# Three adding transfers in place of two for the low parts of an up slab, in a two-layer hybrid decoder trunk

## The chip, the cores and the metric

The kernel runs on one core of a Trainium2 chip. The metric is the device time of one execution, in microseconds (us); lower is better. Before the change the median of three runs is 1875.01 us (1873.65 to 1876.04).

## The reference, cut to what matters

The model has two layers over 528 tokens (16 learned meta tokens and 512 input tokens) of width 1024. Each layer is a mixing half (a convolution branch beside differential attention, gated and projected) and an MLP. Only the MLP is touched by the change:

```python
u = rms_norm(h, norm_mlp[l])
h = h + jnp.square(jax.nn.relu(u @ w_up[l])) @ w_down[l]     # w_up 1024 x 4096, w_down 4096 x 1024
...
return h[:, N_META:N_META + S]
```

All weights are float32. The kernel gets that precision from a faster matmul type (fp32r): a weight w is held as a high part, w rounded to fp32r, and a low part, w minus its high part, and so are the activations. A product is then three matmuls: high x high, high x low, low x high.

## The kernel before, in words

**Slabs.** All weights come as slabs of 1 MB (128 partitions x 2048 float32), 144 over both layers, by one transfer each into one of two buffers of `w_raw` (L604). A slab's high parts go to `w_hi`, its low parts to `w_lo`. In the MLP of a layer four groups g = 0..3 follow each other, each with four up slabs (m = 0..3) and then four down slabs (d = 0..3). Slab m uses buffer m % 2 everywhere.

**Up slabs.** An up slab holds four blocks of weights of 256 KB (QUAD = 512 columns each). `up_products` (L846, matmuls on L883) multiplies them in Winograd's form of Strassen's scheme: seven products in place of eight, in the order p1, p5, p2, p6, p7, p4, p3. Each product is 12 matmuls (four chunks of the inner dimension, three matmuls each), so a slab is 84. p1 takes block 0 of `w_hi`/`w_lo`, p5 block 1, p2 block 2, p6 block 3. The other three products take `x_hi`/`x_lo`, which hold three further blocks: a plain one, then two sums. PE (TensorE) waits for the low parts, for the high parts (`w_form`) and for the sums of the slab before (`u2_done`) ahead of p1; for `p1_done` (ACT's copy of p1) ahead of p6; for `late_low` (the first of the two summed blocks in `x_lo`) ahead of p7; and for `w_ready` (all of `x_lo`) ahead of p3.

**Low parts of an up slab.** ACT (ScalarE) writes minus the weights into `w_lo` (`early_neg`, L1224 for three blocks, L1225 for the last, which is a sum `s2` made by DVE). Later ACT writes `w_hi` (`early_high`, L1230 and L1231). POOL (GpSimd) then issues, in `early_low` (L728), transfers that add the weights to `w_lo` in flight, with rounding to fp32r: w_lo = fp32r(-w) + w. Ahead of them it runs a tiny instruction `tick` (L734) and waits for it. The other low parts, `x_lo`, are subtractions on POOL itself: `late_parts` (L738, L747), four instructions of 128 columns for the plain block and eight for the two sums. POOL's order in a group g > 0 is written out (L750 to L770): early_low(1), plain(1), early_low(2), sums(1), plain(2), early_low(3), sums(2), plain(3) and sums(3), then the four down slabs' low parts (L634, 16 subtractions each), then early_low and late_parts of slab 0 of the next group.

**What waits for the low parts.** Both transfers of a slab signal the semaphore `low_landed[b]`, 16 each. PE waits for both ahead of p1 (L852). SP (SyncE) waits for both at L597, and for `w_form`, `late_low` and `sum_late`, before it loads slab m + 2 into the same buffer of `w_raw`. DVE (VectorE) makes the sums `s2` (L1960, L1961) once a slab has landed, and the sums `s34` for `x_lo` (L1972, L1973) once POOL has read the ones before. ACT's work around a slab of the up stage is, in order: first_product (L1252), hidden_high of the slab before (L1258, L1259), late_plain (L1238), early_high, early_neg of the slab after the next, late_sums (L1244), hidden_high. `down_high` (L1325) follows for the down slabs.

Of the kernel before, what the change touches and what calls it, by code (L numbers as in the profile page):

```python
# [26 lines left out]
ALU = mybir.AluOpType  # L27
# [27 lines left out]
SLAB = NT * 2 * P  # L55
# [14 lines left out]
QUAD = SLAB // 4  # L70
# [209 lines left out]
def build(nc, x_t, w_slabs, pvecs, rows_in, ident_in, mask_in, identb_in, out, h_spill, r_rows):  # L280
    ctx = ExitStack()
    with ctx:
        sem = lambda name: ctx.enter_context(nc.semaphore(name))
# [71 lines left out]
        s2 = at("s2", [P, 2, QUAD], F32, c); c += 2 * QUAD * 4  # L355
# [9 lines left out]
        w_raw = at("w_raw", [P, 2, SLAB], F32, r_w)  # L365
# [78 lines left out]
        u_raw, t_raw, f_hi, f_ready = sem("u_raw"), sem("t_raw"), sem("f_hi"), sem("f_ready")  # L444
        sum_early, sum_late, sums_read = sem("sum_early"), sem("sum_late"), sem("sums_read")
        w_neg, w_form, w_late = sem("w_neg"), sem("w_form"), sem("w_late")
        low_landed, late_low = [sem("low_landed0"), sem("low_landed1")], sem("late_low")
        q_full, p1_done, u2_done, c22_done, tile_sum, relu_done = (sem(x) for x in ("q_full", "p1_done", "u2_done", "c22_done", "tile_sum", "relu_done"))
        v_chain, a_chain, p_chain = sem("v_chain"), sem("a_chain"), sem("p_chain")

# [119 lines left out]
        @block.sync  # L570
        def _(sp):
            slabs = w_slabs.rearrange("(i b) p c -> b i p c", b=2)
            for k, landed in enumerate(h_landed):
                if k in (1, 2):
                    half = slice((k - 1) * SLAB // 2, k * SLAB // 2)
                    sp.dma_start(w_raw[:, 0, half], slabs[0, 0, :, half]).then_inc(w_landed[0] if k == 2 else half_landed, 16)
                sp.dma_start(h[:, 2 * k:2 * k + 2, :], x_t[:, 2 * k:2 * k + 2, :]).then_inc(landed, 16)
            for dst, src in ((ident, ident_in), (maskb, mask_in), (identb, identb_in)):
                sp.dma_start(dst[:], src).then_inc(in_landed, 16)
            sp.dma_start(w_raw[:, 1, :], slabs[1, 0]).then_inc(w_landed[1], 16)  # L580

            def load_slabs(first, last):

                with sp.Fori(first // 2, last // 2) as i:
                    for b in range(2):
                        sp.wait_ge(w_ready, 2 * i + (b - 1))
                        sp.dma_start(w_raw[:, b, :], slabs[b, ds(i, 1)].rearrange("o p c -> p (o c)")).then_inc(w_landed[b], 16)

            start = 2
            for layer in range(LAYERS):  # L590
                load_slabs(start, up_slab(layer, 0, 2))
                for g in range(4):
                    for m in range(8):
                        s = up_slab(layer, g, m + 2)
                        if m < 4:
                            n = up_nth(layer, g, m)
                            sp.wait_ge(low_landed[n % 2], 32 * (n // 2 + 1))  # L597
                            sp.wait_ge(w_form, n + 1)
                            sp.wait_ge(late_low, 2 * n + 1)
                            sp.wait_ge(sum_late, n + 1)  # L600
                        else:
                            sp.wait_ge(w_ready, s - 1)
                        if s < LAYERS * SLABS:
                            sp.dma_start(w_raw[:, s % 2, :], slabs[s % 2, s // 2]).then_inc(w_landed[s % 2], 16)  # L604
                start = (layer + 1) * SLABS + 2
            for i in range(NT):

                sp.wait_ge(h_new, (LAYERS - 1) * NT + i + 1)
                sp.dma_start(out[:, i, :], h[:, i, META:T]).then_inc(stored, 16)
            sp.wait_ge(stored, 16 * NT)  # L610
# [3 lines left out]
        def _(pool):  # L614
# [73 lines left out]
            for layer in range(LAYERS):  # L688
                s0 = layer * SLABS + S_QKV
                splits(done, s0 // 2)  # L690
                split(0, s0 // 2)
                split(1, s0 // 2)
                taps = head_taps(layer)
                for s in range(s0 + 2, s0 + N_QKV + 2):
                    pair, x = (s - 2 - s0) // 3, (s - 2 - s0) % 3 - 1

                    if x == 0:
                        if pair:

                            pool.wait_ge(p_ready, layer * HEADS + 2 * pair - 1)  # L700
                        turn(layer, pair, 0)
                    elif x == 1:

                        pool.wait_ge(scaled, layer * 4 + pair + 1)
                        turn(layer, pair, 1)

                        if pair in (1, 2):
                            pool.wait_ge(roped, (layer * 4 + pair) * 2 + 2)
                    elif pair in range(1, 4):

                        pool.wait_ge(max_ready, (layer * HEADS + 2 * pair - 2) * 3 + 1)
                    split_low(s % 2, s // 2, layer * N_HIGH + s - 1 - s0)
                    if x < 0:
                        for _ in range(4):
                            next(taps, None)
                for _ in taps:
                    pass
                splits((s0 + N_QKV + 2) // 2, (layer * SLABS + S_PW) // 2)
                for m in range(N_PW + N_O):
                    s = layer * SLABS + S_PW + m  # L720
                    split_low(s % 2, s // 2, layer * N_HIGH + N_QKV + m + 1)

                def down_low(g, d):

                    s = down_slab(layer, g, d)
                    split_low(s % 2, s // 2, layer * N_HIGH + N_QKV + N_PW + N_O + 4 * g + d + 1)

                def early_low(g, m):  # L728

                    b, n = m % 2, up_nth(layer, g, m)  # L730
                    pool.wait_ge(w_neg, n + 1)
                    if n > 1:
                        pool.wait_ge(low_landed[b], 32 * (n // 2))
                    chain.link(nc.gpsimd.tensor_tensor(tick[:], ones[:, 0:1], ones[:, 0:1], ALU.mult))  # L734
                    pool.dma_start(w_lo[:, b, 0:3 * QUAD], w_raw[:, b, 0:3 * QUAD], accum_op=ALU.add).then_inc(low_landed[b], 16)
                    pool.dma_start(w_lo[:, b, 3 * QUAD:SLAB], s2[:, b, :], accum_op=ALU.add).then_inc(low_landed[b], 16)

                def late_parts(g, m, parts):  # L738

                    b, n = m % 2, up_nth(layer, g, m)  # L740
                    for k in parts:
                        source = w_raw[:, b, 3 * QUAD:SLAB] if k == 0 else s34[:, (k - 1) * QUAD:k * QUAD]
                        if k < 2:
                            pool.wait_ge(w_late, 2 * n + k + 1)
                        for c in range(0, QUAD, P):
                            cut = slice(k * QUAD + c, k * QUAD + c + P)
                            last = nc.gpsimd.tensor_tensor(x_lo[:, b, cut], source[:, c:c + P], x_hi[:, b, cut], ALU.subtract)  # L747
                        last.then_inc(late_low if k < 2 else w_ready, 1)

                plain, summed = (0,), (1, 2)  # L750
                early_low(0, 0)
                for g in range(4):
                    early_low(g, 1)
                    if g == 0:
                        late_parts(g, 0, plain + summed)
                        late_parts(g, 1, plain + summed)
                        early_low(g, 2)
                    else:
                        late_parts(g, 1, plain)
                        early_low(g, 2)  # L760
                        late_parts(g, 1, summed)
                    late_parts(g, 2, plain)
                    early_low(g, 3)
                    late_parts(g, 2, summed)
                    late_parts(g, 3, plain + summed)
                    for d in range(4):
                        down_low(g, d)
                    if g < 3:
                        early_low(g + 1, 0)
                        late_parts(g + 1, 0, plain + summed)  # L770
                done = (layer + 1) * SLABS // 2
# [3 lines left out]
        def _(pe):  # L775
# [70 lines left out]
            def up_products(layer, g, m):  # L846
# [2 lines left out]
                n2 = span(layer)[1] // 2  # L849
                formed = layer * N_FORMS if (g, m) == (0, 0) else None  # L850
                tiles = (layer * A_TILES + A_MLP + 8 * g) // 2
                pe.wait_ge(low_landed[b], 32 * (n // 2 + 1))  # L852
                pe.wait_ge(w_form, n + 1)
                if n:
                    pe.wait_ge(u2_done, n)
                if formed is not None:
                    pe.wait_ge(f_ready, formed + 2 * KH)
                for k, (f, x, name) in enumerate(PRODUCTS):
                    if name == "p5" and n:
                        pe.wait_ge(c22_done, n)  # L860
                    if name == "p6":
                        pe.wait_ge(p1_done, n + 1)
                    elif name == "p2" and m < 2:
                        if (g, m) == (0, 1):
# [1312 lines left out]
```

## Time and profile before

| what | value |
|---|---|
| median of three runs | 1875.01 us |
| the profiled execution's own time | 1878.18 us |
| span of that execution | 1876.4 us |
| PE busy | 1806.8 us, 96% of the span |
| POOL busy | 1173.1 us, 63% |
| mean granted TensorE clock | 0.991 of full speed |
| adding transfers | 32 of 768 KB and 32 of 256 KB |

The span runs from the first to the last instruction of the profiled execution, and the busy times are sums over it. The eight up stages (four groups in each of two layers) start at some 578, 678, 771 and 862 us in layer 0 and 1502, 1601, 1691 and 1781 us in layer 1. An up stage takes 45 to 53 us, a down stage about 45.

### The profile page before, as it was taken

To read this page: it belongs to the slowest core of one execution; us is meant where nothing else is said; L and a number is where in the kernel's file an instruction comes from. 1 tells how busy PE (TensorE), PEld (TensorE's weight loads), DVE (VectorE), ACT (ScalarE), POOL (GpSimd) and SP (SyncE) were. 2 spreads that over 40 slices of the span, in tenths; PEclk is the share of its full clock that TensorE was granted. 3 is DMA by queue.
4 is the path that set the end of the run, shared out by engine and by line. 5 is a ranking of instruction groups with operands and counts; after the bars stand their busy time and mean duration, and the time that the engine had idled before them with its cause. 6 is when DMAs were issued, how large, how long until landed. Compare 5 with 4: busy or idle time off the path is not lost.

```text
span 1876.4 us, 34787 instructions
## 1 busy us (share of the span) xinstructions
PE 1806.8 (96%) x13053; PEld 1650.9 (88%) x13053; DVE 1311.5 (70%) x2085; ACT 823.4 (44%) x1745; POOL 1173.1 (63%) x2240
## 2 busy tenths in 40 slices
PE   9999999999997999999999999999999989999989
PEld 8999888889997999999999998887678788888787
DVE  7998888777456555646569989888865664647462
ACT  4135565436246343535421355553453563525260
POOL 4777445546774666666687664446477566676664
PEclk9999999999998999999999999999999989999999
DMA  4222111112325463637432221111233362736362
GB/s 176 90 91 68 30 62 46 64 50 92 137 90 137 132 159 113 166 104 173 135 113 90 88 71 46 46 49 65 67 108 126 106 151 99 178 107 164 116 159 85
DMA packets 34794, 194.54 MB, mean 104 GB/s; under 512 B 4048, under 2 KB 4432, under 8 KB 16992
## 3 DMA queue, kind: packets, MB, share of 16 engines
q1 hardware_dynamic: 21888, 147.01, 22.9%
q0 software_dynamic: 9216, 33.56, 9.6%
q10 hardware_dynamic: 3552, 12.15, 1.8%
q8 instruction: 84, 1.38, 0.3%
q14 instruction: 54, 0.44, 0.1%
HBM read 154.85 MB, written 4.29 MB: 85 GB/s over the span
## 4 chain that ended last, share of the span: by engine, by line
PE 69%; POOL 10%; DVE 7%; DMA 5%; ACT 4%; issue 4%; DVEq 0%; POOLq 0%; ACTq 0%
PE psum L789 40%; PE psum L928 13%; PE psum L883 4%; POOL w_lo L634 3%; DMA w_lo<-s 3%; POOL w_lo L627 3%; PE psum L1025 2%; PE psum L993 2%; DMA w_raw<-w_slabs 2%; PE psum L942 2%; POOL x_lo L747 2%; PE psum L1013 1%; ACT e L1343 1%; DVE h L2103 1%; PE psum L1070 1%
## 5 line engine op out<-in xcount | busy, mean ns | idle before, releaser
L634 POOL TENSOR_TENSOR w_lo<-w_raw,w_hi 128x128 fp32r<-128x128 f32 x1152 | 560.6, 525 | 222.5 <-ACT w_hi L1325 194.3
L789 PE MATMUL psum<-u,w_hi 128*128 128x264 f32 (+1 forms) x2112 | 407.7, 308 | 9.1 <-POOL w_lo L627 5.0
L789 PEld LDWEIGHTS psum<-u,w_hi 128*128 128x128 f32 x2112 | 310.0, 189 | 31.5 <-POOL w_lo L627 6.5
L789 PE MATMUL psum<-hid,w_hi 128*128 128x264 f32 (+1 forms) x1536 | 328.3, 322 | 5.7 <-POOL w_lo L634 5.7
L560 DVE SCALAR_TENSOR_TENSOR psum<-xg,pvec,psum 128x512 f32<-128x512 f32 x440 | 301.0, 750 | 4.6 <-DVE xg L1815 2.2
L928 PE MATMUL psum<-w_hi,u 128*128 128x256 f32 x1536 | 287.7, 287 | 0.1
L789 PEld LDWEIGHTS psum<-hid,w_hi 128*128 128x128 f32 x1536 | 237.3, 188 | 30.3 <-issue 7.0
L789 PE MATMUL psum<-u,w_lo 128*128 128x264 f32 (+1 forms) x1056 | 251.2, 304 | 0.0
L928 PEld LDWEIGHTS psum<-w_hi,u 128*128 128x128 f32 x1536 | 237.6, 189 | 10.7 <-issue 10.3
L627 POOL TENSOR_TENSOR w_lo<-w_raw,w_hi 128x128 fp32r<-128x128 f32 x480 | 237.4, 532 | 2.5
L928 PE MATMUL psum<-w_lo,u 128*128 128x256 f32 x768 | 215.9, 281 | 0.0
L1325 ACT CAST w_hi<-w_raw 128x2048 fp32r<-128x2048 f32 x72 | 137.4, 1908 | 173.8 <-PE psum L789 173.8
L789 PE MATMUL psum<-hid,w_lo 128*128 128x264 f32 (+1 forms) x768 | 204.8, 321 | 0.0
L883 PE MATMUL psum<-uh,w_hi 128*128 128x264 f32 (+1 forms) x512 | 152.6, 298 | 36.6 <-DMA w_lo<-s 15.8
L789 PEld LDWEIGHTS psum<-u,w_lo 128*128 128x128 f32 x1056 | 170.6, 189 | 8.5
L2102 DVE TENSOR_TENSOR down_tmp<-psum,r_inv 128x512 f32<-128x512 f32 (+1 forms) x56 | 39.1, 699 | 165.9 <-PE psum L789 165.7
L883 PE MATMUL psum<-ul,w_hi 128*128 128x264 f32 (+1 forms) x512 | 148.4, 290 | 0.0
L883 PE MATMUL psum<-uh,w_lo 128*128 128x264 f32 (+1 forms) x512 | 148.1, 289 | 0.0
L928 PEld LDWEIGHTS psum<-w_lo,u 128*128 128x128 f32 x768 | 145.4, 189 | 0.0
L747 POOL TENSOR_TENSOR x_lo<-s,x_hi 128x128 fp32r<-128x128 f32 x256 | 127.7, 906 | 22.7 <-ACT x_hi L1244 22.7
L883 PEld LDWEIGHTS psum<-uh,w_hi 128*128 128x128 f32 x512 | 100.4, 196 | 42.6 <-DMA w_lo<-s 17.8
L789 PEld LDWEIGHTS psum<-hid,w_lo 128*128 128x128 f32 x768 | 127.7, 188 | 11.2
(253 smaller groups left out, 3606.6 us busy)
## 6 DMA issues: line engine op xcount, KB each, us to landing
w_raw<-w_slabs SPq DMA_DIRECT2D x135, 1024.0 KB, 4.9
w_lo<-w_raw POOLq DMA_DIRECT2D x32, 768.0 KB, 5.9
w_lo<-s POOLq DMA_DIRECT2D x32, 256.0 KB, 6.8
h<-x_t SPq DMA_DIRECT2D x4, 528.0 KB, 7.3
h<-x_t ACTq DMA_DIRECT2D x1, 2112.0 KB, 9.5
h_spill<-h ACTq DMA_DIRECT2D x8, 264.0 KB, 2.7
h<-h_spill ACTq DMA_DIRECT2D x1, 2112.0 KB, 8.4
out<-h SPq DMA_DIRECT2D x8, 256.0 KB, 2.2
```

Of the source, the lines that this page charges most:

```text
L560: return nc.vector.scalar_tensor_tensor(out=done if ends else acc, in0=x, scalar=w, in1=done if begins else acc, op0=ALU.mult, op1=ALU.add)
L627: last = nc.gpsimd.tensor_tensor(w_lo[:, b, c:c + P], w_raw[:, b, c:c + P], w_hi[:, b, c:c + P], ALU.subtract)
L634: last = nc.gpsimd.tensor_tensor(w_lo[:, b, c:c + P], w_raw[:, b, c:c + P], w_hi[:, b, c:c + P], ALU.subtract)
L747: last = nc.gpsimd.tensor_tensor(x_lo[:, b, cut], source[:, c:c + P], x_hi[:, b, cut], ALU.subtract)
L789: last = nc.tensor.matmul(psum[:, 2 * slot + j, 0:n], w[:, b, cut], src[:, part, kc, at0:at0 + n], start=(kc == 0 and m == 0), stop=(kc == ...
L883: last = nc.tensor.matmul(quad(layer, m, name), w[:, cut], act_[:, x, kc, 0:n2], start=(kc == 0 and j == 0), stop=(kc == KH - 1 and j == 2))
L928: done = nc.tensor.matmul(psum[0:tn, B_BANK[n], 0:2 * P], u[:, part, kc, t0:t0 + tn], w[:, b, kc * 2 * P:(kc + 1) * 2 * P], start=k == 0, ...
L942: last = nc.tensor.matmul(psum[0:2 * META, bank, 0:2 * P], meta_u[:, kc, :], w[:, b, kc * 2 * P:(kc + 1) * 2 * P], start=kc == 0 and w is ...
L993: nc.tensor.matmul(psum[0:tn, banks[c], at0:at0 + k1 - k0], qk[rows64, 0, hh % 2, qp, t0:t0 + tn], qk[rows64, 1, hh % 2, kp, k0:k1], start ...
L1025: last = nc.tensor.matmul(psum[:, bank, (i - 1) * P:SEQ], v_sb[0:kn, hh // 2 % 2, j, cut], a_t[0:kn, b0:b0 + n, :].rearrange("p a b -> p ( ...
L1325: nc.scalar.copy(w_hi[:, b, :], w_raw[:, b, :]).then_inc(w_high, 1)
L2102: announce(dve, V.tensor_tensor(row(down_tmp[:], layer), a_ps(layer, j), row(r_inv2[:], layer), ALU.mult), a_free[j], a_read(layer, A_MLP ...
```

## The change

The 1 MB of low parts of an up slab is added by three transfers of 256, 512 and 256 KB (blocks 0, 1 and 2, 3), each with a semaphore of its own for each buffer, in place of two transfers of 768 and 256 KB with one. PE waits for the first ahead of p1, for the second ahead of p5, for the third ahead of p6. SP and POOL wait for all three where they waited for both.

```diff
-        low_landed, late_low = [sem("low_landed0"), sem("low_landed1")], sem("late_low")
+        low_landed, late_low = [[sem(f"low_landed{b}{part}") for part in "abc"] for b in range(2)], sem("late_low")
...
-                            sp.wait_ge(low_landed[n % 2], 32 * (n // 2 + 1))
+                            for landed in low_landed[n % 2]:
+                                sp.wait_ge(landed, 16 * (n // 2 + 1))
...
                     if n > 1:
-                        pool.wait_ge(low_landed[b], 32 * (n // 2))
+                        for landed in low_landed[b]:
+                            pool.wait_ge(landed, 16 * (n // 2))
                     chain.link(nc.gpsimd.tensor_tensor(tick[:], ones[:, 0:1], ones[:, 0:1], ALU.mult))
-                    pool.dma_start(w_lo[:, b, 0:3 * QUAD], w_raw[:, b, 0:3 * QUAD], accum_op=ALU.add).then_inc(low_landed[b], 16)
-                    pool.dma_start(w_lo[:, b, 3 * QUAD:SLAB], s2[:, b, :], accum_op=ALU.add).then_inc(low_landed[b], 16)
+                    pool.dma_start(w_lo[:, b, 0:QUAD], w_raw[:, b, 0:QUAD], accum_op=ALU.add).then_inc(low_landed[b][0], 16)
+                    pool.dma_start(w_lo[:, b, QUAD:3 * QUAD], w_raw[:, b, QUAD:3 * QUAD], accum_op=ALU.add).then_inc(low_landed[b][1], 16)
+                    pool.dma_start(w_lo[:, b, 3 * QUAD:SLAB], s2[:, b, :], accum_op=ALU.add).then_inc(low_landed[b][2], 16)
...
-                pe.wait_ge(low_landed[b], 32 * (n // 2 + 1))
+                pe.wait_ge(low_landed[b][0], 16 * (n // 2 + 1))
...
-                    if name == "p5" and n:
-                        pe.wait_ge(c22_done, n)
+                    if name == "p5":
+                        pe.wait_ge(low_landed[b][1], 16 * (n // 2 + 1))
+                        if n:
+                            pe.wait_ge(c22_done, n)
                     if name == "p6":
+                        pe.wait_ge(low_landed[b][2], 16 * (n // 2 + 1))
                         pe.wait_ge(p1_done, n + 1)
```

## Rows read from the trace of the kernel before

**Rows 1.** The page: busy share of PE and the others, and the chain by line.

```profile
PE 1806.8 (96%) x13053; PEld 1650.9 (88%) x13053; DVE 1311.5 (70%) x2085; ACT 823.4 (44%) x1745; POOL 1173.1 (63%) x2240
PE psum L789 40%; PE psum L928 13%; PE psum L883 4%; POOL w_lo L634 3%; DMA w_lo<-s 3%; POOL w_lo L627 3%; PE psum L1025 2%; PE psum L993 2%; DMA w_raw<-w_slabs 2%; PE psum L942 2%; POOL x_lo L747 2%; PE psum L1013 1%; ACT e L1343 1%; DVE h L2103 1%; PE psum L1070 1%
```

**Rows 2.** Waits of the span: engine, line, releaser, us in total, times, longest.

```profile
PEld psum L883 <- DMA w_lo<-s: 17.8, 9, 5.7
```

**Rows 3.** Chain of waits, first up stages of both layers: start us, us, what.

```profile
582.54 4.93 POOL x_lo L747 x8
...
587.52 4.64 PE psum L883 x36
...
593.05 5.84 PE psum L883 x48
...
602.05 6.58 DMA w_lo<-s
...
608.67 22.96 PE psum L883 x168
...
1533.15 22.72 PE psum L883 x168
1555.87 4.19 PE psum L789 x18
```

**Rows 4.** Chain of waits in layer 0's third up stage.

```profile
774.65 6.77 DMA w_lo<-s
...
781.44 8.68 DMA w_raw<-w_slabs
...
794.24 0.87 POOL w_lo L735
795.11 0.90 POOL w_lo L736
796.00 3.39 POOL x_lo L747 x8
```

**Rows 5.** Timeline of POOL: start us, us, engine, line, what, idle before and releaser.

```profile
602.05 1.19 POOL L736 DMA_DIRECT2D w_lo<-s  x1
...
609.68 3.98 POOL L747 TENSOR_TENSOR x_lo<-s,x_hi 128x128 fp32r<-128x128 f32 x8
...
711.76 3.39 POOL L747 TENSOR_TENSOR x_lo<-s,x_hi 128x128 fp32r<-128x128 f32 x8 [1.72 <-ACT x_hi L1244]
...
1534.22 3.98 POOL L747 TENSOR_TENSOR x_lo<-s,x_hi 128x128 fp32r<-128x128 f32 x8
```

**Rows 6.** DMA issues at 600 to 604 us: KB each, us to landing.

```profile
w_lo<-w_raw POOLq DMA_DIRECT2D x1, 768.0 KB, 5.8
w_lo<-s POOLq DMA_DIRECT2D x1, 256.0 KB, 6.6
```

**Rows 7.** The same at 604 to 609.5 us, and POOL's queue over the span.

```profile
w_lo<-s POOLq DMA_DIRECT2D x1, 256.0 KB, 11.8
q0 software_dynamic: 9216, 33.56, 9.6%
```

**Rows 8.** Windows of PE: stretch, us, PE busy (instructions), granted clock, DMA share, GB/s.

```profile
587.50:592.00 4.50, 4.48 (x37) 1.00 0.66 238
608.70:614.00 5.30, 5.30 (x25) 0.52 0.81 194
1512.80:1515.20 2.40, 2.40 (x14) 0.55 0.36 150
```

**Rows 9.** Timelines of PE and of ACT.

```profile
587.52 0.39 PE L883 MATMUL psum<-uh,x_hi 128*128 128x264 f32 x1 [0.92 <-POOL x_lo L747]
608.67 0.59 PE L883 MATMUL psum<-uh,w_hi 128*128 128x264 f32 x1 [5.42 <-DMA w_lo<-s]
690.20 0.39 PE L883 MATMUL psum<-uh,w_hi 128*128 128x264 f32 x1 [1.49 <-DMA w_lo<-s]
1510.73 0.38 PE L883 MATMUL psum<-uh,x_hi 128*128 128x256 f32 x1 [1.74 <-POOL x_lo L747]
...
602.57 0.61 ACT L1231 CAST w_hi<-s 128x512 fp32r<-128x512 f32 x1
609.45 0.65 ACT L1259 ACTIVATE hid<-relu 128x528 fp32r<-128x528 f32 x1
```

## The prediction

> **What bounds the kernel now.** The page first: PE is busy for 1806.8 of 1876.4 us, and matmul lines hold most of the chain; adding transfers hold 3% of it, POOL's `x_lo` 2% [rows 1]. So little is to be had, and it lies where PE stands still. The list of waits says how much of that is the transfers' doing: 17.8 us in nine waits at L883 [rows 2]. PE's timeline shows where these nine are: 5.42 us ahead of slab 2 of group 0 in layer 0 and as much (5.5) in layer 1, 1.49 ahead of slab 1 of group 1 in layer 0 and under 1 in each of the others [rows 9]. Last the chain of waits, because a wait that is shortened only pays where nothing else comes behind it. In the first up stage of a layer it runs POOL `x_lo` (x8) -> PE -> the landing of slab 2's low parts -> PE [rows 3]. In the later ones it runs past PE: landing of slab 1's low parts -> load of slab 3 into the freed buffer (8.68 us) -> ACT and POOL for slab 3, the two issues of 0.87 and 0.90 us among them -> `x_lo` -> DVE -> slab 3 [rows 4]. That second chain needs all low parts, not the first of them.
>
> **The prices.** A full-clock product is 12 x 5.84 / 48 = 1.46 us [rows 3].
>
> *When the parts land.* The two transfers issued at 601.47 and 602.05 us land 5.8 and 6.6 us after their issues, at 607.3 and 608.65, that is 5.8 and 7.2 us after the first issue [rows 6]. The last 256 KB thus takes 1.35 us; 768 KB at that rate takes 4.1 and leaves 1.7 us ahead of the first byte's work. POOL's queue moves 33.56 MB in 9.6% of the span: 180 us over 32 slabs, 5.6 us a slab, 1.4 for each 256 KB, the same [rows 7]. After the change: first part at 1.7 + 1.4 = 3.1 us, second at 5.9, third at 7.3. The third is issued 1.2 to 1.8 us after the first, long before the engines get to it, so it costs the last landing about nothing. Bounds for the first part: 1.7 us (nothing moved) and 7.2 (all parts end together). I take 3.1, since the two parts of today land in turn.
>
> *What a third issue costs POOL.* POOL goes on 0.56 us after the start of L736, but L736 lasts 1.19 [rows 5], and the chain puts 0.90 us to it [rows 4]. The eight `x_lo` subtractions right behind it take 3.98 us, against 3.39 after an idle time [rows 5]: they catch 0.6 us of its tail. So an issue costs 0.89 us of POOL in full, 0.57 if only the dispatch counts, 1.19 at most. I take 0.89, the figure that both readings give. It is paid 32 times; where POOL has idle time it is hidden.
>
> *Waits.* Two more on PE for each slab, on SP and on POOL two more: PE reads ahead, and between products that have a wait today (p5's, p2's) the pace is the 1.46 us of the others. Nothing, at most 0.1 us a slab where POOL has just been released.
>
> **Group 0, the gain.** Slab 0 starts when ACT has written `w_hi`, four us after the low parts would let it: no gain. But its p7 waits for `x_lo`, 0.92 us in layer 0 and 1.74 in layer 1 [rows 9], and that `x_lo` stands right behind slab 1's issues [rows 3]. The third issue delays it in full: +0.89 in each layer. All of slab 1, and the issue for slab 2, move with it.
> Slab 2: PE is free at 603.25 + 0.89. The high parts are there at 603.2 + 0.89 (L1231) [rows 9]. First part: 601.47 + 0.89 + 3.1 = 605.5, so p1 starts there and not at 608.67. p5 at 608.3 (second part), p2 at 609.7. p6 needs the third part (609.7) and ACT's copy of p1, which stands behind L1259: 610.10 + 0.89 + 0.4 = 611.4 [rows 9]. p7 needs the first half of the sums in `x_lo`: before at 609.68 + 3.98 - 4 x 0.42 = 611.98 (3.39 / 8 = 0.42 each), now later by its own slab 3's third issue and the shift, 613.8 [rows 5]. p7 started at 631.63 - 120 x 0.1217 = 617.0 [rows 3]. Gain 3.3 us with the shift counted in. In layer 1: 1534.22 + 3.98 - 1.68 + 1.78 = 1538.3 against 1555.87 - 120 x 0.119 = 1541.6, again 3.3 [rows 3, 5]. A part of it is the clock: today slab 2's first 5.3 us run at a granted 0.52, the 1.2 GHz level, after 5.4 us without work [rows 8]; two gaps of 1.3 us in its place should mostly keep the 2.4 GHz. POOL is what binds then, so more clock would give no more.
> Nothing takes it back: slab 3's last part lands at 609.12 + 11.8 + 0.89 = 621.8 [rows 7] (it competes with a load), and slab 3's p6 is at 618.3 + 4.4 = 622.7; unsplit it would have held p1 at 618.3. POOL's L634 for the first down slab follows `x_lo` of slab 3 and is done at about 627 against PE's 628.4.
> One more cost: slab 0's gap in layer 0 grows from 0.92 to 1.8 us. After the 0.92 the clock stays at 1.00; after layer 1's 1.74 it falls to 0.55, worth 1.6 us over three products [rows 8, 9]. Between 0 and 1.6, I take 0.8. Group 0 in all: -(3.3 - 0.8) - 3.3 = -5.8 us.
>
> **Groups 1 to 3, the loss.** The chain holds slab 3's issues, and the third adds 0.89 in full: `x_lo`, DVE's sums, u2_done for slab 3 and the down slab's L634 all stand behind it [rows 4]. Slab 1's last part, for which SP holds the load of slab 3, lands as before. PE's earlier start of slab 1 is hidden behind that load, but for layer 0's group 1, where DVE is busy until it starts on the landed slab and the 1.49 us [rows 9] give back up to 0.9: there gain and loss cancel. The issues of slabs 0, 1 and 2 fall into idle time of POOL (0.7 to 4 us ahead of `tick`). Five stages x 0.89 = +4.5 us.
>
> **The sum.** -5.8 + 4.5 = -1.3 us on the profiled execution's 1878.18 us: 1876.9. The median of the runs is 3.2 us below that execution, so 1873.7 us. What a measurement here can tell from no change is 0.2%, 3.75 us: the forecast is no change.
>
> **A rule that speaks against it.** The second transfer's landing 1.35 us after the first's shows no fixed part paid again [rows 6]. The Trainium skill, "DMA: Bandwidth & Descriptors", section "Anatomy of one DMA", gives a transfer from GpSimd about 2.0 us fixed plus its bytes at 436 GB/s, with half efficiency near 860 KB. By its figures, paid in turn, the three would take 2.6 + 3.2 + 2.6 = 8.4 us against 3.8 + 2.6 = 6.4, an estimate by that page; if its fixed parts overlap, it agrees with the trace. The mechanism is rival B.
>
> **Rivals.**
> *A, faster: the third issue costs POOL its dispatch only.* For: POOL starts the next instruction 0.56 us after L736's start. Against: that work ends late. Then group 0 gives 617.0 - (611.98 + 2 x 0.57) = 3.9 in each layer, without the clock's loss, and the five stages cost 5 x 0.57 = 2.9: -4.9, 1870.1 us. A load of slab 3 that lands sooner between finer transfers (8.68 us here) would lead the same way.
> *B, slower: the last part lands later.* Price: the 1.7 us ahead of the first byte once more for the third transfer. Place: the landing of slab 1's parts, which SP's load awaits, in five stages. 5 x 1.7 - 1.3 = +7.2, 1882.2 us. It decides from (3.75 + 1.3) / 5 = 1.0 us a stage. For: the load follows the landing within 0.02 us [rows 4]. Against: 1.35 us between the landings of today.
> *C, slower: it doesn't do what it says,* the parts share the engines and the first lands with the last. Group 0 then loses 2 x 0.89 + 0.8 and gains nothing, +2.6 + 4.5 = +7.1, 1882.1 us. Against: equal numbers of rows are in both transfers of today, and they land in turn.
>
> **How the numbers follow.** No change 0.45, A 0.30, B 0.15, C 0.10. So faster 0.30, same 0.45, slower 0.25. The forecast's own range is 1871.3 to 1878.7; the range to hold 8 times in 10 reaches past A (issue at 0.57, full clock) and to B and C: 1868.5 to 1882.5.
>
> **What would show it.** Right: two PE gaps of 1.3 us ahead of p1 and p5 of slab 2 in both first stages, with the clock near 1.00 and down stages that start 2.5 to 3.3 us sooner after their slab 0; first parts landing about 3 us after issue, last ones at 7.3; in later stages the time from slab 3's `tick` to the first down matmul longer by 0.9. Wrong: last parts at 8 us or more (B), first ones near 7 (C), the eight `x_lo` behind the issues no later than 0.6 us (A), or a POOL that stands on the third issue longer than 1.2 us.

## The result: 0.42% slower, and the profile after

The changed kernel takes 1882.53 us, the median of five runs (1879.85 to 1885.23). The kernel before takes 1875.01 us (1872.95 to 1876.04, five runs). The ratio is 1.0042, 95% interval 1.0027 to 1.0056. The forecast was no change, 1873.7 us, and its range ended at 1882.5, so the result lies just past its end.

First the page of the kernel after. Its lines answer to [rows 1] and to [rows 7].

```profile
PE 1804.6 (96%) x13053; PEld 1648.3 (88%) x13053; DVE 1308.0 (70%) x2085; ACT 823.3 (44%) x1745; POOL 1208.9 (64%) x2272
q0 software_dynamic: 13824, 33.56, 10.1%
PE psum L792 40%; PE psum L934 13%; POOL w_lo L635 3%; POOL x_lo L750 3%; DMA w_raw<-w_slabs 3%; POOL w_lo L628 3%; PE psum L1031 2%; PE psum L999 2%; DMA w_lo<-s 2%; PE psum L948 2%; PE psum L1019 1%; DVE h L2109 1%; ACT e L1349 1%; ACT w_hi L1331 1%; PE psum L889 1%
w_lo<-w_raw POOLq DMA_DIRECT2D x32, 512.0 KB, 5.6
w_lo<-w_raw POOLq DMA_DIRECT2D x32, 256.0 KB, 3.4
w_lo<-s POOLq DMA_DIRECT2D x32, 256.0 KB, 6.6
```

POOL is busy for 36 us more, and the chain has moved from the adding transfers (2% now) to POOL's `x_lo` (3%) and the others. The queue's engine time grew by little (10.1% of the span). The first 256 KB land 3.4 us after their issue: the early signal is there. The last part lands 6.6 us after its own issue. Counted from the first issue of its slab it comes a little later than before: 7.4 us in place of 7.1 in slab 0 of groups 1 to 3, and 7.9 in place of 7.4 in slab 1, whose landing the load of slab 3 awaits (means of six slabs, from the DMA rows of both traces). So the transfers did nearly what was planned, and most of the time went elsewhere.

Stage by stage, from PE's timeline: from the first matmul of an up stage to the first of its down stage, in us.

| up stage | L0 g0 | g1 | g2 | g3 | L1 g0 | g1 | g2 | g3 | sum |
|---|---|---|---|---|---|---|---|---|---|
| before | 53.06 | 45.48 | 44.63 | 45.31 | 54.00 | 45.79 | 45.18 | 46.24 | 379.7 |
| after | 52.49 | 45.88 | 46.67 | 46.49 | 53.65 | 45.80 | 47.35 | 46.61 | 384.9 |

In this pair of executions group 0 gained 0.6 and 0.35 us, and groups 1 to 3 lost 6.2 together. The profiled execution of before took 1878.18 us, 3.2 over its median, and that of after, 1879.85, is the fastest of its five. That is why the two spans differ by 1.6 us and the medians by 7.5. A stretch that the change does not touch, from the start of layer 0's last down stage to layer 1's first up stage, took 594.3 us before and 591.4 after, so one trace against another says little on a few us, and the verdicts below rest on the timed runs.

How far the stages can be trusted shows where a later experiment left them alone. Groups 1 to 3 add up to 272.6 us in the trace of before and to 272.9 in that of e3, which leaves them as before. They add up to 278.8 in that of after and to 281.1 in that of e13, which leaves them as changed: a loss of 6 to 8 us. Group 0 of layer 0 with two transfers takes 52.8 to 53.5 us in five traces (before, e4, e6, e7, e8), and changed 52.49 and 52.53 (after, e14): a gain of some 0.5 us. In layer 1 the 54.00 us of before stand alone: the same two-transfer stage takes 51.3 to 51.7 us in the other four traces. Changed it takes 53.65 and 52.16 us (after, e14). So the 0.35 us above are no gain, and in layer 1 group 0 more likely lost by the change.

Group 0 of layer 0 in PE's timeline of the kernel after (idle before and releaser in brackets), to be set against [rows 9]:

```profile
605.17 0.39 PE L889 MATMUL psum<-uh,w_hi 128*128 128x264 f32 x1 [1.64 <-DMA w_lo<-w_raw]
607.91 0.39 PE L889 MATMUL psum<-uh,w_hi 128*128 128x264 f32 x1 [1.00 <-DMA w_lo<-w_raw]
613.83 0.36 PE L889 MATMUL psum<-uh,x_hi 128*128 128x264 f32 x1 [0.85 <-POOL x_lo L750]
624.16 0.36 PE L889 MATMUL psum<-uh,w_hi 128*128 128x264 f32 x1 [0.70 <-ACT r_inv L1258]
630.80 0.36 PE L792 MATMUL psum<-hid,w_hi 128*128 128x264 f32 x1 [0.58 <-POOL w_lo L635]
```

The first three lines are slab 2's p1, p5 and p7: forecast 605.5, 608.3 and 613.8, and there they are, within 0.4 us. The 5.42 us of idle time before have become 1.64 + 1.00, with 0.85 ahead of p7 behind them. The clock stayed up, as a window of slab 2 shows (stretch, us, PE busy, granted clock, DMA share, GB/s), where [rows 8] had 0.52:

```profile
605.20:610.50 5.30, 4.30 (x33) 1.00 0.91 154
```

But slab 3's p6 waits for ACT's copy of p1 until 624.16, and the down stage starts at 630.80, not at 628.4. What is ahead of that copy, in the timelines of POOL, ACT and DVE (kernel after; `...` marks a change of place or engine):

```profile
609.32 0.87 POOL L737 DMA_DIRECT2D w_lo<-w_raw  x1 [0.30 <-POOL tick L736]
609.90 1.18 POOL L738 DMA_DIRECT2D w_lo<-w_raw  x1
610.44 1.53 POOL L739 DMA_DIRECT2D w_lo<-s  x1
611.00 4.33 POOL L750 TENSOR_TENSOR x_lo<-s,x_hi 128x128 fp32r<-128x128 f32 x8
...
623.82 6.73 POOL L635 TENSOR_TENSOR w_lo<-w_raw,w_hi 128x128 fp32r<-128x128 f32 x16 [1.70 <-ACT w_hi L1331]
...
620.66 0.61 ACT L1264 ACTIVATE relu<-psum 128x528 f32<-128x528 f32 x1 [2.00 <-DVE psum L2028]
...
621.86 1.89 ACT L1331 CAST w_hi<-w_raw 128x2048 fp32r<-128x2048 f32 x1
623.65 0.36 ACT L1258 COPY r_inv<-psum 128x264 f32<-128x264 f32 x1
...
615.43 1.28 DVE L1978 TENSOR_TENSOR s<-w_raw,s 128x512 f32<-128x512 f32 x1 [2.55 <-POOL x_lo L750]
...
620.19 0.44 DVE L2028 TENSOR_TENSOR psum<-psum,q_u 128x264 f32<-128x264 f32 x1
```

Read it as a chain. POOL's three issues take it to 611.97, so its sums of slab 2 are done at 615.33 (611.00 + 4.33). DVE stood idle for 2.55 us for them. It combines the products of slab 2 behind them in its queue, up to L2028 at 620.19. ACT's relu waits for that; then ACT writes the down slab's high parts, at 621.86, and only then copies p1, for which PE waits. POOL's L635 waits for the same high parts, is done at 630.55, and holds the first product of the down stage. Before the change ACT wrote these high parts at 621.77, 0.5 us after slab 3's p1 had started at 621.27. With p1 at the forecast's 618.3 it would have been 618.8, an estimate from these two figures. So the 2.6 us by which slab 3 started sooner (618.68 in place of 621.27) moved the high parts by nothing. Layer 1 shows the same waits in the trace of after: 0.71 us ahead of p6 for ACT's copy, 0.72 ahead of the down stage for POOL's L635.

The chain of waits in the third up stage of layer 0, the kernel after, against [rows 4]:

```profile
774.85 6.73 DMA w_lo<-s
...
781.70 9.60 DMA w_raw<-w_slabs
...
795.42 0.87 POOL w_lo L737
796.30 0.90 POOL w_lo L738
797.19 0.89 POOL w_lo L739
798.08 3.37 POOL x_lo L750 x8
...
807.98 1.90 ACT w_hi L1331
...
809.95 6.75 POOL w_lo L635 x16
...
816.93 41.13 PE psum L792 x336
```

It is the same chain with one more link of 0.89 us, and it ends in the first product of the down stage, as before. Two smaller things stand in it as well. Slab 1's last part lands 7.85 us after the slab's first issue (774.85 + 6.73, first issue at 773.73), before 7.35, and SP's two further waits put 0.12 us between that landing and the load, before 0.02.

### The profile page after: what moved, and what is told of

Same layout as the page of the kernel before. It is cut to its first block, busy times and chain, and to the rows that moved or that the text cites. A ratio compares the mean times of both kernels' runs of the same rounds, so it can differ in the third digit from the quotient of the medians.

```text
span 1878.0 us, 34942 instructions
## 1 busy us (share of the span) xinstructions
PE 1804.6 (96%) x13053; PEld 1648.3 (88%) x13053; DVE 1308.0 (70%) x2085; ACT 823.3 (44%) x1745; POOL 1208.9 (64%) x2272
## 3 DMA queue, kind: packets, MB, share of 16 engines
q0 software_dynamic: 13824, 33.56, 10.1%
## 4 chain that ended last, share of the span: by engine, by line
PE 64%; POOL 12%; DVE 8%; issue 5%; DMA 5%; ACT 5%; DVEq 0%; POOLq 0%; ACTq 0%; SPq 0%
PE psum L792 40%; PE psum L934 13%; POOL w_lo L635 3%; POOL x_lo L750 3%; DMA w_raw<-w_slabs 3%; POOL w_lo L628 3%; PE psum L1031 2%; PE psum L999 2%; DMA w_lo<-s 2%; PE psum L948 2%; PE psum L1019 1%; DVE h L2109 1%; ACT e L1349 1%; ACT w_hi L1331 1%; PE psum L889 1%
## 5 line engine op out<-in xcount | busy, mean ns | idle before, releaser
L635 POOL TENSOR_TENSOR w_lo<-w_raw,w_hi 128x128 fp32r<-128x128 f32 x1152 | 563.3, 528 | 212.8 <-ACT w_hi L1331 184.6
L792 PEld LDWEIGHTS psum<-u,w_hi 128*128 128x128 f32 x2112 | 309.4, 188 | 31.2 <-POOL w_lo L628 6.5
L750 POOL TENSOR_TENSOR x_lo<-s,x_hi 128x128 fp32r<-128x128 f32 x256 | 136.3, 1132 | 18.6 <-ACT x_hi L1250 18.6
```

The source lines that it names most:

```text
L635: last = nc.gpsimd.tensor_tensor(w_lo[:, b, c:c + P], w_raw[:, b, c:c + P], w_hi[:, b, c:c + P], ALU.subtract)
L792: last = nc.tensor.matmul(psum[:, 2 * slot + j, 0:n], w[:, b, cut], src[:, part, kc, at0:at0 + n], start=(kc == 0 and m == 0), stop=(kc == ...
```

## The experiments

Each was timed in five rounds beside the kernel before, 5 to 12 executions of each; the kernel before had medians of 1874.74 to 1875.41 us beside them. "By part" means that PE waits for a transfer's signal ahead of the first product that reads its blocks. The cuts of code under e1 and e2 show what the edits come to; the runs' own code goes by the helpers shown under e3.

| kernel | median us | ratio to before, 95% interval |
|---|---|---|
| after (the change) | 1882.53 | 1.0042 (1.0027 to 1.0056) |
| e1 three, all ahead of p1 | 1885.67 | 1.0051 (1.0036 to 1.0066) |
| e2 two, by part | 1873.42 | 0.9988 (0.9977 to 0.9999) |
| e3 three in slab 2 of group 0 | 1878.70 | 1.0017 (1.0007 to 1.0026) |
| e4 three in slab 3, groups 1 to 3 | 1878.60 | 1.0014 (1.0003 to 1.0025) |
| e5 three in slabs 2 and 3 of group 0, by part | 1874.31 | 0.9997 (0.9988 to 1.0006) |
| e6 before, and 0.84 us more of POOL | 1879.76 | 1.0025 (1.0016 to 1.0033) |
| e7 three in slab 1, groups 1 to 3 | 1876.44 | 1.0004 (0.9992 to 1.0016) |
| e8 three in slab 2, groups 1 to 3 | 1876.34 | 1.0004 (0.9996 to 1.0013) |
| e9 after, reordered | 1869.72 | 0.9968 (0.9958 to 0.9979) |
| e10 e2, reordered | 1874.98 | 0.9996 (0.9985 to 1.0008) |
| e11 three in slab 3, by part, reordered | 1865.78 | 0.9949 (0.9932 to 0.9966) |
| e12 e2, three in slab 2 of group 0 | 1877.92 | 1.0008 (0.9998 to 1.0018) |
| e13 after, reordered in group 0 only | 1881.89 | 1.0040 (1.0026 to 1.0054) |
| e14 after, reordered in groups 1 to 3 only | 1869.69 | 0.9976 (0.9964 to 0.9988) |
| e15 e11, three in slab 2 of group 0 | 1860.85 | 0.9925 (0.9912 to 0.9938) |

**e1, the costs without the early start.** Against the changed kernel, whose waits ahead of p5 and p6 go:

```diff
-                pe.wait_ge(low_landed[b][0], 16 * (n // 2 + 1))
+                for part in range(3):
+                    pe.wait_ge(low_landed[b][part], 16 * (n // 2 + 1))
```

> All 32 up slabs by three transfers, but PE waits for all three ahead of p1: the costs of the change without its early start. Theory 1 (the third issue costs POOL 0.9 us on slab 3's chain, and the slab 3 load is slower beside more and smaller transfers): groups 1 to 3 as in the changed kernel, group 0 without its gain of about 0.5 us a layer and with 0.9 us more: 8 to 11 us above before. Theory 2 (the new waits on PE cost the time, by the gaps ahead of p6): 0 to 3 us above before.

1.0051: the cost is there, some 10 us, with no new wait between products. Theory 2 falls. The changed kernel's ratio is lower by 0.0009, which the two intervals do not tell apart, so the early start is not shown to be worth anything in it.

**e2, the waits without the third issue.** Against the kernel before, with a semaphore for each of the two transfers:

```diff
-                pe.wait_ge(low_landed[b], 32 * (n // 2 + 1))
+                pe.wait_ge(low_landed[b][0], 16 * (n // 2 + 1))
...
                     if name == "p6":
+                        pe.wait_ge(low_landed[b][2], 16 * (n // 2 + 1))
```

> Two transfers as before, each with a signal of its own; PE waits for the 768 KB ahead of p1 and for the 256 KB ahead of p6. No third issue. Theory 1: no cost anywhere, slab 2 of group 0 starts 1.3 us sooner, clock recovered in part: 1 to 4 us below before. Theory 2 (waits on PE cost): not below before.

0.9988: the waits by part cost nothing and gain a little, about 2 us.

**e3, one slab a layer.** `in_three(g, m)` says which slabs go by three transfers, and `by_part(g, m)`, here and in e4, e7 and e8 the same condition, for which of them PE waits by part; the others go by two, with both awaited ahead of p1.

```diff
+                    cuts = [(0, 0, 1), (1, 1, 3)] if in_three(g, m) else [(0, 0, 3)]
+                    for part, q0, q1 in cuts:
+                        pool.dma_start(w_lo[:, b, q0 * QUAD:q1 * QUAD], w_raw[:, b, q0 * QUAD:q1 * QUAD], accum_op=ALU.add).then_inc(low_landed[b][part], 16)
...
+    return (g, m) == (0, 2)
```

> Only slab 2 of group 0 (one slab a layer) by three transfers with waits by part, all others as before. Theory 1: p7 of that slab is released by x_lo at 612.0 us in place of 616.9, the stage ends 2.5 to 4.5 us sooner in each layer, 4 to 9 us below before. Rival (DVE's order behind the sums of x_lo holds the stage's end, whatever PE does): at most 1 us a stage, 0 to 2 us below before.

A miss on both theories: it is slower, by 3 to 4 us. The slab started early, but here is slab 3's p1 in PE's timeline of this kernel:

```profile
622.83 0.36 PE L913 MATMUL psum<-uh,w_hi 128*128 128x264 f32 x1 [4.22 <-DMA w_lo<-s]
```

PE was done with slab 2 at 618.6 and stood until slab 3's last part had landed, 11.8 us after its issue beside the load of a down slab, as in [rows 7]. Before the change that landing was hidden. Starting one slab sooner turned it into the next wait, the clock fell again (0.56 granted over slab 3's p1, which took 2.5 us), and the gain was gone. In layer 1 the same wait is 3.18 us.

**e4, e7, e8, which slab of groups 1 to 3 pays.** The same edit with these conditions:

```diff
+    return g > 0 and m == 3      # e4
+    return g > 0 and m == 1      # e7
+    return g > 0 and m == 2      # e8
```

> Only slab 3 of groups 1 to 3 by three transfers (six slabs). Theory 1, POOL's share: 0.9 us in each of six stages, 4 to 6 us above before, slab 2's p6 gap as before. Rival (the loss is in the load that waits for slab 1's last part and competes with slab 2's transfers): under 1.5 us above before.

> Only slab 1 of groups 1 to 3 by three transfers (six slabs), with waits by part. Its last part releases the load of slab 3. If the last part lands later by 0.4 to 0.5 us, as in the one stage of the changed kernel that I read: 2 to 4 us above before. If it lands as before: within 1 us of before.

> Only slab 2 of groups 1 to 3 by three transfers (six slabs), with waits by part. They compete with the load of slab 3. If more transfers slow that load (9.6 us against 8.7 in the one stage that I read): 3 to 6 us above before. If not: within 1 us of before.

Slab 3's third issue costs 0.14%, 2.6 us by the ratio and 3.5 by the medians: above the rival's 1.5, and short of the 4 to 6 that theory 1 gave. Slab 1's and slab 2's cost 0.04% each, with intervals that hold no change and, at their ends, 2.4 and 3 us. So the timed runs don't say whether the later landing of slab 1's last part (7.7 us from the first issue in e7, 7.4 before) costs anything. The load of slab 3 takes from 6.4 to 10.4 us over the six stages and all traces. In the stage shown above it took 8.7 us in before, e3 and e6, and 9.6 to 9.7 in after, e7, e9, e13 and e14; but e1, with three transfers, has 8.5 there, and e10, with two, 10.4. In the last up stage of layer 1 it went the other way, from 10.2 us in before to 7.9 in after. Over the six stages it adds up to 54.3 us before and 53.1 after. So the load makes the stages uneven, and is not shown to make their sum longer.

**e6, POOL's time alone.** The kernel before, with two subtractions behind slab 3's two issues:

```diff
+                    if g and m == 3:
+                        for k in range(2):
+                            nc.gpsimd.tensor_tensor(spare[:, k * P:k * P + P], ones[:], ident[:], ALU.subtract)
```

> The kernel before with two subtractions of 128 columns on POOL (0.42 us each, into unused memory) right behind slab 3's two issues in groups 1 to 3, six times; no third transfer. If POOL's time alone is what the third issue of slab 3 costs: 3 to 5 us above before, as slab 3 alone in three (3.6 above). If the transfers themselves cost: under 1.5 us above before.

1.0025, 4.7 us by the ratio (interval 3.0 to 6.2) and 4.4 by the medians, for 6 x 0.84 = 5.0 us of POOL. POOL's time at this place goes to the end of the run almost in full, with no transfer added. In the timeline of POOL, third up stage of layer 0:

```profile
796.67 1.19 POOL L737 DMA_DIRECT2D w_lo<-s  x1
797.23 1.53 POOL L740 TENSOR_TENSOR spare<-ones,ident 128x128 f32<-128x128 f32 x2
798.07 3.97 POOL L751 TENSOR_TENSOR x_lo<-s,x_hi 128x128 fp32r<-128x128 f32 x8
```

**e5, e12, early start in group 0 with waits by part.** `in_three` as below, and waits by part in every slab.

```diff
+    return g == 0 and m > 1      # e5
+    return (g, m) == (0, 2)      # e12
```

> Slabs 2 and 3 of group 0 by three transfers, all other slabs by two; PE waits by part in every slab. Theory (the early start of slab 2 pays once slab 3 need not wait for its last part, which lands some 12 us after its issue beside the load of a down slab): 3 to 7 us below before, below the kernel with two transfers by part (1873.4). Rival (POOL's third issue ahead of slab 2's sums, and DVE behind them, take it back): 0 to 2.5 us below before, no better than two by part.

> Two transfers by part everywhere, but slab 2 of group 0 by three. If the early start of slab 2 is worth something when no other slab pays for it: 2 to 4 us below two by part (1873.4). If slab 3's 768 KB, which lands some 10.4 us after its issue beside a load, holds its p1 as its last part did in the run with slab 2 alone: equal to two by part within 1 us.

Neither is faster than e2, and e5 is as its rival had it. In e12 slab 3's p1 waits 2.7 us for its 768 KB in layer 0; in e5 the third issue of slab 3 stands ahead of slab 2's sums. e12 misses both of its expectations: it is above even its rival's (1.0008 against e2's 0.9988), and why by so much isn't settled.

**e9, the third issue off the chain.** The changed kernel, with POOL's order turned round:

```diff
-                    late_parts(g, 2, plain)
+                    late_parts(g, 2, plain + summed)
                     early_low(g, 3)
-                    late_parts(g, 2, summed)
```

> The changed kernel (32 slabs by three transfers) with one edit: POOL issues slab 3's transfers behind the sums of slab 2 in x_lo in place of ahead of them. If the change's cost is POOL time ahead of those sums: the three issues (2.7 us) leave the chain, of which ACT's x_hi (ready 0.9 us after the point where POOL started its issues) keeps some 1; 1.2 to 1.8 us in each of eight stages, 9 to 14 us below the changed kernel, 1869 to 1874. If slab 3's low parts, which now are issued 3.5 us later, hold PE: 1876 to 1884.

> Two transfers by part (1873.4) with the same reordering. Without it the two issues (1.8 us) stand ahead of the sums; gain 0.8 to 1.0 us a stage, 6 to 8 below it, unless slab 3's 768 KB, which lands 5.9 us after an issue at the end of the sums, holds its p1: that would be some 1.5 us later than PE is free, and take it back: 1872 to 1875. I expect the second.

> The reordering, with slab 3 of every group by three transfers and the others by two, PE waits by part everywhere. The first part of slab 3 lands 3.1 us after its issue, in time for p1, and no third issue stands ahead of a product's wait: the reordering's gain is kept. 1864 to 1870, the fastest of all.

All three as expected. Reordered, the changed kernel is 12.8 us faster than it was and 0.32% faster than before. POOL in the third up stage of layer 0 of e9:

```profile
792.16 3.37 POOL L750 TENSOR_TENSOR x_lo<-s,x_hi 128x128 fp32r<-128x128 f32 x8 [8.72 <-ACT x_hi L1249]
795.48 0.20 POOL L736 TENSOR_TENSOR tick<-ones 128x1 f32<-128x1 f32 x1
795.98 0.87 POOL L737 DMA_DIRECT2D w_lo<-w_raw  x1 [0.30 <-POOL tick L736]
```

The sums now start as soon as ACT's part is there and end 29.6 us after the stage's first matmul (795.53, stage start 765.96), where the changed kernel had 31.2 (801.45, 770.26). With two transfers (e10) the same order gives nothing: slab 3's 768 KB then land late, and its p1 waits 0.9 to 2.5 us for them in groups 1 to 3; with three in slab 3 alone (e11) it gives 0.51%.

**e13, e14, which groups, and e15, the best.** The same reordering under `if g == 0` and under `if g > 0`, and e11 with `m == 3 or (g, m) == (0, 2)`.

> The changed kernel with the reordering in group 0 of each layer only. If POOL's three issues ahead of slab 2's sums, with DVE and ACT behind them, held group 0's gain: its stage in both layers 2 to 2.5 us shorter, 4 to 5 us below the changed kernel, 1877 to 1879. If slab 3's late landing or the clock held it: within 2 us of the changed kernel's 1882.5.

> The changed kernel with the reordering in groups 1 to 3 only. By the same mechanism 1.2 to 1.8 us in each of six stages: 7 to 10 us below the changed kernel, 1872 to 1875; the two runs together account for what the reordering in all groups gave (12.8).

> The fastest so far (reordering, slab 3 of every group by three, 1865.8) with slab 2 of group 0 by three as well. If the early start of slab 2 now pays: 2 to 4 us below it, 1862 to 1864. If slab 3's p1, which waits for its first part in group 0, takes it back: 1865 to 1868.

e14 gives it all: 1869.69, 12.8 us below the changed kernel, more than the 7 to 10 expected, and the excess isn't explained. e13 gives 0.6 us, not 4: the rival's range. In its trace the stage of layer 0 takes 50.37 us against 52.49, with no wait of slab 3's p6 left and 0.97 us ahead of its p5. In layer 1 it takes 52.74 against 53.65, because slab 3's second part, now issued later beside a load, holds p5:

```profile
1541.43 0.38 PE L893 MATMUL psum<-uh,w_hi 128*128 128x256 f32 x1 [2.45 <-DMA w_lo<-w_raw]
```

The 3 us that these stages show do not show in the medians, whose intervals are 2.6 us wide to each side. Layer 1's 52.74 is no shorter than the 52.16 of e14, where group 0 is as in the changed kernel, so only layer 0's 2.1 us are a gain in more than one pair of traces; what the reordering of group 0 is worth stays open. e15 is the best of all, 1860.85 us, 0.75% below before and 4.9 us below e11, more than the 2 to 4 expected (by the ratios 0.24%, with intervals that just touch). So the early start of slab 2 does pay once neither POOL's order nor slab 3's landing takes it back. In its layer 0 group 0 takes 49.89 us, in layer 1 49.59.

## Why the prediction was wrong

**The prices were right.** The first part lands 3.4 us after its issue (forecast 3.1), the last 7.4 us after the first issue where nothing disturbs it (forecast 7.3); a third issue is a link of 0.89 us (forecast 0.89). Rival A, 0.57 us an issue, falls with that link. Rival B's 1.7 us did not come: the last part came 0.3 us later in slab 0 and 0.5 later in slab 1 of groups 1 to 3, where the forecast had "lands as before". Rival C falls, since the first part came early. That B and C had 1882.2 and 1882.1 us, near the 1882.5 measured, is chance: neither mechanism was there at that size. The rule of the Trainium skill, "DMA: Bandwidth & Descriptors", section "Anatomy of one DMA", of 2.0 us fixed for each transfer, would give 8.4 us for the three if paid in turn, an estimate by that page. The 7.4 us measured do not bear that out.

**Slab 0's p7 in group 0:** +0.89 in each layer forecast; the wait grew from 0.92 to 1.40 and from 1.74 to 2.26 us, and the clock of slab 0 did not fall in layer 0. Smaller than forecast. That the fall to 0.55 in layer 1 came of the 1.74 us gap does not hold either: e6 has a gap of 1.73 us at the same place, and the granted clock of the 4.5 us behind it is 1.00, where before it is 0.62.

**Slab 2 in group 0:** right to 0.4 us at p1, p5, p6 and p7, clock included.

**The step that failed** is "Nothing takes it back". It followed PE, the landing of slab 3 and POOL's L634, and left out DVE, which was taken to follow PE. DVE's sums for slab 3 stand ahead of its combining of slab 2 and wait for POOL's sums of slab 2, which the forecast itself had 1.8 us later. With slab 2 early, DVE was no longer behind PE but PE behind DVE and ACT. The time for L634 was wrong for the same reason: "done at about 627" let it follow `x_lo` of slab 3, but already before the change it waited for ACT's high parts, which stand behind DVE's combining. The timeline of POOL before:

```profile
623.74 6.74 POOL L634 TENSOR_TENSOR w_lo<-w_raw,w_hi 128x128 fp32r<-128x128 f32 x16 [3.63 <-ACT w_hi L1325]
```

It ended at 630.48 before and at 630.55 after. Group 0 gave 0.9 us in this pair of traces and not 5.8, and by the other traces less than that. e9 has slab 3's issues behind those sums, and its layer 0 down stage starts at 628.37, the forecast's 628.4. The traces show this chain at the end of group 0 in both layers of the changed kernel. In e9 and e13 it is gone, and in layer 1 slab 3's second part, which then lands late, takes its place with 2.4 us ahead of p5. What either is worth in timed runs e13 left open.

**Groups 1 to 3: the mechanism was right, the size was small.** "Five stages x 0.89 = +4.5" came out as 6.2 in the trace of after and 8.4 in that of e13. The stages do not share it evenly, from 0.0 to 2.2 us each in the trace of after, and the loads of slab 3, longer in some and shorter in others, go with that. e6 and e4 show the mechanism: POOL time ahead of slab 2's sums goes into the total at 0.7 to 0.8 us a stage (e6) for 0.84 put in, and slab 3's third issue costs 2.6 to 3.5 us by itself (e4). e14 shows that this place is worth more than the third issue: with all three issues out of it, 12.8 us. The term put at nothing was slab 1's landing, 0.5 us later in the mean with 0.1 more at SP. It points the right way, but the timed run of slab 1 alone (e7) does not resolve it. In group 1 of layer 0, where gain and loss were to cancel, the stage lost 0.4.

**The sum:** -1.3 forecast, 7.5 measured (5 to 10 by the interval). In the traces groups 1 to 3 lost 6 to 8 us, group 0 gained some 0.5 in layer 0 and lost up to 2 in layer 1, and that covers the 7.5. For the 6 to 8, five stages of 0.89 for the issue and 0.65 for slab 1's landing and SP make 7.7, an estimate from the traces. The timed runs do not separate these: e4, e7 and e8 add up to 0.22% of the 0.42%, and the third issues of slab 0, and of slab 1 in group 0, were not run by themselves.

## What to carry to other kernels

A transfer from POOL's queue has two prices, its landing and the 0.9 us that its issue takes from POOL; here the second went to the total almost in full (e6), and the earlier landing paid nothing as long as other work held the same stage. So a split pays where the issues stand behind the work that others wait for: the same 32 third issues cost 0.42% in one order and came with a gain of 0.32% in the other, in which two transfers gained nothing (e10). And a wait removed on one engine has to be followed through the queue of every other engine for the next slab too: here DVE and ACT, and in e3 a landing that used to be hidden, took the gain back.

## What the runs showed of the hardware

POOL starts an instruction 0.54 to 0.58 us after the start of a DMA issue (after, 609.32 to 611.00), but the instruction's results come 0.9 us later for each issue ahead of it. With two, three and no issues ahead, eight subtractions took 3.98 us (before, 609.68), 4.33 (after, 611.00) and 3.39 (before, 711.76) from their first start, and the chain has links of 0.87, 0.90 and 0.89 us for three issues of 256, 512 and 256 KB.

Three adding transfers issued one behind the other land 3.4, 6.1 and 7.4 us after the first issue, two of 768 and 256 KB 5.9 and 7.1 (slab 0 of groups 1 to 3). A load of 1 MB that starts beside 1 MB of adding transfers (before, 608.6) finishes in 6.4 us, against the page's median of 4.9, and the last adding transfer lands 11.8 us after its issue, against 6.6 for slab 2's.

An idle time of 1.73 or 1.74 us of PE at the same place was followed by 4.5 us at a granted clock of 1.00, the 2.4 GHz level, in e6 and of 0.62 in before.
